# Where the first norm factor is applied, and how x is loaded and split, in a two-layer decoder step

## The reference, cut to what matters

```python
def rmsnorm(x, w):
    y = x * lax.rsqrt(jnp.mean(x * x, axis=-1, keepdims=True) + NORM_EPS)
    return y * w
...
h = rmsnorm(x, norm_w[0])                       # 320 tokens x 2048
proj = h @ w_in                                 # q, k, v, z and 2 x 32 gate columns
qkv, z, beta_raw, a_raw = jnp.split(proj, ...)
qkv = silu(causal_conv(qkv, cache, conv_w))     # width 4
o = gated_delta_rule(l2norm(q), l2norm(k), v, g(a_raw), sigmoid(beta_raw), state)
x = x + (rmsnorm(o) * silu(z)) @ w_out          # then the pooling layer and a last rmsnorm
```

## Time and profile before

| | |
|---|---|
| time, median of 3 runs | 2062.27 us |
| span of the profiled execution | 2061.9 us |
| TensorE (PE) busy | 2039.8 us, 99% |
| VectorE (DVE) busy | 1253.5 us, 61% |
| ScalarE (ACT) busy | 939.3 us, 46% |
| GpSimd (POOL) busy | 156.5 us, 8% |
| DMA, mean | 151 GB/s |

### The profile page before, as it was taken

One profiled execution on the slowest core, in us unless ns is written; L12 is line 12 of the kernel. 1 busy time (PEld: TensorE's weight loads), 2 busy tenths in 40 slices (PEclk: granted clock), 3 DMA queues, 4 the chain that ended last, 5 costly groups with the idle time before them and its releaser, 6 DMA issues.

```text
span 2061.9 us, 51677 instructions
## 1 busy us (share of the span) xinstructions
PE 2039.8 (99%) x19467; PEld 1959.5 (95%) x19467; DVE 1253.5 (61%) x2238; ACT 939.3 (46%) x2005; POOL 156.5 (8%) x354
## 2 busy tenths in 40 slices
PE   8999999999999999999999999999999999999998
PEld 7999999999999999999899999999999999999998
DVE  5766677776667776667754445555556556744433
ACT  5555555564555555455543334333333333433343
POOL 4101011010011101101100010000000000000010
PEclk9999999999999999999999999999999999999999
DMA  6544555554555554455555445454544445444443
GB/s 203 166 133 136 162 153 153 152 144 122 144 162 156 150 148 137 125 163 152 159 166 162 134 152 171 147 160 144 161 157 141 150 154 161 157 155 143 150 138 110
DMA packets 380491, 311.13 MB, mean 151 GB/s; under 512 B 19945, under 2 KB 377018, under 8 KB 379834
## 3 DMA queue, kind: packets, MB, share of 16 engines
q1 hardware_dynamic: 378554, 306.30, 49.0%
q10 hardware_dynamic: 1872, 3.96, 0.6%
HBM read 283.85 MB, written 27.25 MB: 151 GB/s over the span
## 4 chain that ended last, share of the span: by engine, by line
PE 93%; DVE 5%; issue 1%; ACT 0%; DVEq 0%; POOL 0%; ACTq 0%; POOLq 0%
PE ps L297 28%; PE ps L298 26%; PE ps L299 26%; PE ps L1227 10%; DVE s_s L1164 2%; PE ps L1382 2%; DVE wlo L288 1%; DVE silu L1019 1%; DVE silu L1017 1%; DVE amat L1174 1%; PE ps L1353 0%; DVE xlo L896 0%; PE ps L1356 0%; DVE sq L903 0%; PE ps L2030 0%
## 5 line engine op out<-in xcount | busy, mean ns | idle before, releaser
L297 PE MATMUL ps<-xhi,whi 128*128 128x320 f32 x3072 | 983.8, 320 | 5.8 <-DVE wlo L288 2.6
L299 PE MATMUL ps<-xhi,wlo 128*128 128x320 f32 x3072 | 949.6, 309 | 0.0
L298 PE MATMUL ps<-xlo,whi 128*128 128x320 f32 x3072 | 949.4, 309 | 0.0
L288 DVE TENSOR_TENSOR wlo<-wraw,whi 128x1024 fp32r<-128x1024 f32 (+1 forms) x484 | 579.1, 1217 | 240.2 <-ACT whi L283 237.7
L283 ACT ACTIVATE whi<-wraw 128x1024 fp32r<-128x1024 f32 (+1 forms) x484 | 498.0, 1050 | 307.8 <-PE ps L299 276.7
L297 PEld LDWEIGHTS ps<-xhi,whi 128*128 128x128 f32 x3072 | 577.4, 188 | 30.5 <-issue 15.9
L298 PEld LDWEIGHTS ps<-xlo,whi 128*128 128x128 f32 x3072 | 577.9, 188 | 0.9
L299 PEld LDWEIGHTS ps<-xhi,wlo 128*128 128x128 f32 x3072 | 577.3, 188 | 0.0
L297 PE MATMUL ps<-bhi,whi 128*128 128x320 f32 x512 | 157.7, 308 | 0.0
L298 PE MATMUL ps<-blo,whi 128*128 128x320 f32 x512 | 157.6, 308 | 0.0
L299 PE MATMUL ps<-bhi,wlo 128*128 128x320 f32 x512 | 157.6, 308 | 0.0
(11 more groups left out here) (352 smaller groups left out, 2048.1 us busy)
## 6 DMA issues: line engine op xcount, KB each, us to landing
wraw<-in_delta_w_in_dram SPq DMA_DIRECT2D x384, 256.0 KB, 3.0
wraw<-in_pool_w_in_dram SPq DMA_DIRECT2D x256, 256.0 KB, 3.0
wraw<-in_delta_w_out_dram SPq DMA_DIRECT2D x128, 256.0 KB, 3.3
wraw<-in_pool_w_out_dram SPq DMA_DIRECT2D x128, 256.0 KB, 3.3
s_s<-in_state_delta_dram SPq DMA_DIRECT2D x32, 512.0 KB, 6.2
out_dram<-s_s SPq DMA_DIRECT2D x32, 512.0 KB, 4.2
wraw<-in_pool_w_group_dram SPq DMA_DIRECT2D x64, 256.0 KB, 3.2
dec<-gc_rows SPq DMA_DIRECT2D x16, 320.0 KB, 4.0
```

The costliest lines, as they stand in the source:

```text
L288: nc.vector.tensor_tensor(wlo[:, slot, 0:width], wraw[:, slot, 0:width], whi[:, slot, 0:width].bitcast(F32), ALU.subtract).then_inc(E("w_l ...
L297: mm(o, whi[:, slot, w], hi[:, k_x, :], start=first, stop=False)
L298: mm(o, whi[:, slot, w], lo[:, k_x, :], start=False, stop=False)
L299: done = mm(o, wlo[:, slot, w], hi[:, k_x, :], start=False, stop=last)
```

## The change

It makes `xhi` on ScalarE straight from the turned tile in PSUM, scaled by the weight of the norm, and `xlo` on VectorE from `ht`, the weight and `xhi`; `sq` goes. `rb` is made behind the first eight k tiles of head 0 and multiplied where a projection leaves PSUM, for which `gfeat`, `qk_evac`, `v_evac` and `z_evac` become products on VectorE, at new places in its list. x is loaded in three pieces of columns, the small rows through ScalarE's DMA queue; the sums of squares stand between the tiles; GpSimd's constants for the level work wait for x; the gate chain stands four k tiles later, and VectorE's splits around it move. In the loop VectorE's last split of a turn (`split(11)`) moves behind the branch rows.

```diff
-    BY_DVE = (1, 3, 5, 7)
+    BY_ACT = (2, 4, 6, 8, 10, 12)
+    BY_DVE = (0, 1, 3, 5, 7, 9, 11, 13, 14, 15)
+    X_COLS = ((0, 4), (4, 10), (10, KT))
     def tile_bank(k):
...
-                "j (n c) -> (j n) c", c=P)).then_inc(E("rows_in"), 16)
-        sp.dma_start(gvec[:, 0, :], delta_a_log[0].partition_broadcast(P)).then_inc(E("rows_in"), 16)
-        sp.dma_start(gvec[:, 1, :], delta_dt_bias[0].partition_broadcast(P)).then_inc(E("rows_in"), 16)
+        for c, (c0, c1) in enumerate(X_COLS):
+            cols = slice(P * c0, P * c1)
+            sp.dma_start(xtok[:, 0, cols], x_prompt[0, 0:P, cols]).then_inc(E(f"x_in{c}"), 16)
+            sp.dma_start(xtok[:, 1, cols], x_prompt[0, P:2 * P, cols]).then_inc(E(f"x_in{c}"), 16)
...
         gp.tensor_copy(level[:], lv[:]).then_inc(E("c_all"), 1)
...
-            act.wait_ge(E("tiles_t"), k + 1)
-            sc.activation(ht[:, k, :], tile_bank(k)[:, 0:T], ACT.Copy).then_inc(E("act_tiles"), 1)
+        for s, r, n in ((norm_w.rearrange("n (k c) -> (n k) c", c=P), 0, 32),
...
+        act.wait_ge(E("vecs"), 1)
+        for k in range(KT):
+            act.wait_ge(E("tiles_t"), k + 1)
+            sc.activation(xhi[:, k, :], tile_bank(k)[:, 0:T], ACT.Copy, scale=vecs[:, k:k + 1]).then_inc(E("x_hi"), 1)
+            if k in BY_ACT:
+                sc.activation(ht[:, k, :], tile_bank(k)[:, 0:T], ACT.Copy).then_inc(E("act_tiles"), 1)
+            if k >= 12:
+                split_hi(act, k - 12, k - 12, 512)
+            if k in (6, 9, 12):
+                if k == 6:
+                    for c in range(len(X_COLS)):
+                        act.wait_ge(E(f"x_in{c}"), 48)
+                row_squares(k // 3 - 2)
+        split_hi(act, HEADS, 0)
+        act.wait_ge(E("act_tiles"), len(BY_ACT))
+        act.wait_ge(E("dve_tiles"), len(BY_DVE))
+        act.dma_start(ht_dram, ht[:].rearrange("p k t -> p (k t)")).then_inc(E("ht_saved"), 16)
...
-        for k in (2, 4, 6):
-            tile(k)
-        split_hi(act, 0, 0, 512)
-        for k in (8, 9, 10):
-            tile(k)
-        for k in range(KT):
-            if k + 11 < KT:
-                tile(k + 11)
-            if k in (2, 6, 10):
-                n = (k + 2) // 4
-                split_hi(act, n, n, 512)
-            if k == 8:
-                act.wait_ge(E("act_tiles"), 12)
-                act.wait_ge(E("dve_tiles"), 4)
-                act.dma_start(ht_dram, ht[:].rearrange("p k t -> p (k t)")).then_inc(E("ht_saved"), 16)
-            act.wait_ge(E("xnorm"), k + 1)
-            sc.activation(xhi[:, k, :], sq[:, k % 4, :], ACT.Copy).then_inc(E("x_hi"), 1)
-        split_hi(act, HEADS, 0)
-        for j in range(1, 4):
-            split_hi(act, HEADS + j, j)
...
+        for m in range(1, 4):
+            split_hi(act, HEADS + m, m)
...
-            act.wait_ge(E("w_used"), used)
-            if loop_of(i):
-                act.wait_ge(E("conv"), i * 16)
-            sc.activation(convin[:, 0:2, TAPS - 1:S_AT], ps[:, 0:2, 0:NPT], ACT.Copy)
-            sc.activation(conv_strips(convin, 0, 2, TAPS - 1, SLEN), toks(ps[:, 0:2, NPT:T]), ACT.Copy
-                          ).then_inc(E("qk_evac"), 1)
...
-        def z_evac(i, used):
-            act.wait_ge(E("z_half"), i + 1)
-            if loop_of(i):
-                act.wait_ge(E("gate"), i)
-            sc.activation(zraw[:, 0, :], ps[:, 0, 0:T], ACT.Copy)
-            act.wait_ge(E("w_used"), used)
-            sc.activation(zraw[:, 1, :], ps[:, 1, 0:T], ACT.Copy).then_inc(E("z_evac"), 1)
...
+        def low_x(k):
+            dve.wait_ge(E("x_hi"), k + 1)
+            tile_kept(dve, k)
+            v.scalar_tensor_tensor(xlo[:, k, :], ht[:, k, :], vecs[:, k:k + 1], xhi[:, k, :].bitcast(F32),
+                                   ALU.mult, ALU.subtract).then_inc(E("x_lo"), 1)
+        for k in range(KT):
+            if k in BY_DVE:
+                dve.wait_ge(E("x_hi"), k + 1)
+                v.tensor_copy(ht[:, k, :], tile_bank(k)[:, 0:T]).then_inc(E("dve_tiles"), 1)
+            if k >= 1:
+                low_x(k - 1)
+            if k >= 13:
+                split_lo(dve, k - 13, k - 13, 512)
+        low_x(KT - 1)
         dve.wait_ge(E("sumsq"), 3)
         v.tensor_scalar(small[:, 0:2], small[:, 3:5], 1.0 / DM, EPS, ALU.mult, ALU.add)
         v.tensor_scalar(small[0:64, 2:3], small[0:64, 5:6], 1.0 / DM, EPS, ALU.mult, ALU.add).then_inc(E("ms"), 1)
+        split_lo(dve, 3, 3, 512)
+        split_lo(dve, HEADS, 0)
         dve.wait_ge(E("rms"), 1)
         v.reciprocal(small[:, 9:11], small[:, 6:8])
         v.reciprocal(small[0:64, 11:12], small[0:64, 8:9]).then_inc(E("rinv"), 1)
...
+        last.then_inc(E("rms_row"), 1)
+        split_lo(dve, HEADS + 1, 1)
+        split_lo(dve, HEADS + 2, 2)
+        dve.wait_ge(E("row_ps"), 2)
+        v.tensor_copy(rb[:], D3[:, 0:T]).then_inc(E("rms_row"), 1)
+        dve.wait_ge(E("rms_row"), 2)
...
-        v.tensor_copy(gfeat[:], ps[:, 3, 0:T]).then_inc(E("g_in"), 1)
-        split_lo(dve, HEADS + 1, 1)
+        v.tensor_tensor(gfeat[:], ps[:, 3, 0:T], rb[:], ALU.mult).then_inc(E("g_in"), 1)
...
-        split_lo(dve, HEADS + 2, 2)
+        split_lo(dve, HEADS + 3, 3)
         dve.wait_ge(E("g_pe"), 1)
...
-        split_lo(dve, HEADS + 3, 3)
+        split_lo(dve, HEADS + 4, 0)
...
-        split_lo(dve, HEADS + 4, 0)
+        split_lo(dve, HEADS + 5, 1)
...
+        def evacuate(at, i, used, name):
+            dve.wait_ge(E("w_used"), used)
+            dve.wait_ge(E("conv_zero"), 1)
+            if not isinstance(i, int):
+                dve.wait_ge(E("tail"), i)
+            v.tensor_tensor(convin[:, at:at + 2, TAPS - 1:S_AT], ps[:, at:at + 2, 0:NPT],
+                            rb[:, 0:NPT].rearrange("p (o c) -> p o c", o=1).to_broadcast([P, 2, NPT]), ALU.mult)
+            for q in range(at, at + 2):
+                last = v.tensor_tensor(conv_strips(convin, q, q + 1, TAPS - 1, SLEN)[:, 0],
+                                       ps[:, q, NPT:T].rearrange("p (b s) -> p b s", s=SLEN),
+                                       rb[:, NPT:T].rearrange("p (b s) -> p b s", s=SLEN), ALU.mult)
+            last.then_inc(E(name), 1)
+        def qk_evac(i):
+            evacuate(0, i, i * 12 + (HEADS + 4), "qk_evac")
+        def v_evac(i):
+            evacuate(2, i, i * 12 + (HEADS + 8), "v_evac")
+        def z_evac(i):
+            dve.wait_ge(E("z_half"), i + 1)
+            if not isinstance(i, int):
+                dve.wait_ge(E("gate"), i)
+            v.tensor_tensor(zraw[:, 0, :], ps[:, 0, 0:T], rb[:], ALU.mult)
+            dve.wait_ge(E("w_used"), i * 12 + (HEADS + 12))
+            v.tensor_tensor(zraw[:, 1, :], ps[:, 1, 0:T], rb[:], ALU.mult).then_inc(E("z_evac"), 1)
...
-        split_lo(dve, HEADS + 5, 1)
+        split_lo(dve, HEADS + 6, 2)
...
         put(HBETA, ge)
+        qk_evac(0)
         dve.wait_ge(E("g_pe"), 3)
...
-        split_lo(dve, HEADS + 6, 2)
+        split_lo(dve, HEADS + 7, 3)
         dve.wait_ge(E("g_pe"), 4)
         v.tensor_copy(gcr[0:80, :], D1[0:80, 0:P]).then_inc(E("g_vec"), 1)
-        split_lo(dve, HEADS + 7, 3)
...
             v.scalar_tensor_tensor(gate[:], gate[:], 1.0, zraw[:], ALU.add, ALU.mult).then_inc(E("gate"), 1)
             split(3)
+            qk_next()
...
                     v.tensor_copy(xm[BL:64, :, 0:BL], blocks(D2[BL:64, 0:P], 4)).then_inc(E("x5"), 1)
                     split(8)
+            v_next()
...
             states(3)
             silus_next()
-            split(11)
+            z_next()
             dve.wait_ge(E("pe_round"), n + 1)
             b = branch[:, bass.ds(d * 2, 2), :]
             v.scalar_tensor_tensor(b[:, :, 0:NPT], blocks(D0, 2), vecs[:, V_O:V_O + 1], gate[:, :, 0:NPT], ALU.mult, ALU.mult)
             v.scalar_tensor_tensor(b[:, :, NPT:T], blocks(D1[:, 0:P], 2), vecs[:, V_O:V_O + 1], gate[:, :, NPT:T],
                                    ALU.mult, ALU.mult).then_inc(E("dve_round"), 1)
+            split(11)
...
         for half in range(2):
+            if half == 1:
+                split_lo(dve, HEADS + 10, 2)
+                split_lo(dve, HEADS + 11, 3)
             for j in range(TAPS):
                 conv(0, half, j)
-            for j in (10, 11) if half == 0 else range(12, 12 + LEAD):
-                split_lo(dve, HEADS + j, j % 4)
+            if half == 0:
+                v_evac(0)
+        for j in range(12, 12 + LEAD):
+            split_lo(dve, HEADS + j, j % 4)
         silus(0)
         decay_exponents(0)
+        z_evac(0)
...
+        pe.wait_ge(E("vrow_in"), 64)
+        tr(ps[:, 0, 320:321 + V_O], vrow[0:V_O + 1, :], ident[0:V_O + 1, 0:V_O + 1]).then_inc(E("row_ps"), 1)
         for k in range(KT):
...
                 tile_kept(pe, k - 5)
+                pe.wait_ge(E("x_hi"), k - 4)
...
-            if k == 4:
...
                 for h in range(2):
                     last = tr(ps[:, 2, P * h:P * h + P], crow[:, h, :], ident[:])
-            if k == 6:
```

(48 more changed lines are left out.)

96 lines of the change are left out of this document (25 added, 71 removed).

## The result

The changed kernel takes 2069.95 us (median of 6 runs, 2068.89 to 2070.89) against 2062.98 us (6 runs, 2061.71 to 2064.48): a ratio of 1.0032, 95% interval 1.0022 to 1.0041, so slower, by 7.0 us between the medians. The forecast was 2067.3 us, with a range of 2062 to 2071.5; the median lies 2.65 us above it. The profiled executions have spans of 2061.9 and 2067.2 us, 5.3 us apart; the kernel after is profiled in its fastest run (2068.89 us), so the rest of the 7.0 us is what executions of one kernel differ by. In later comparisons the kernel before has medians of 2063.63 to 2064.19 us, so a difference of medians that were not taken together is good to about 1 us. TensorE has as many matmuls as before (19467), behind longer waits.

The account below looks back on a forecast made before the run. TensorE bounds the loop, so only its waits at the start, head 0 and the last head can gain: +3.9 us up to head 1, +0.75 loop, +0.4 last head, +5.0 in all: 2067.3 us (8 in 10: 2062 to 2071.5).

Parts of the forecast that it names:

- T: Start of the first projection tile: from 40.11 to 38.5 us, 1.6 us earlier, with the clock low until 33.7 us.
- Rival 1: At the start the clock holds at 2.4 GHz through the gap, first projection tile at 36.3 us; 2065.1 us, chance 0.17.
- Piece 5: Head 0's projection: TensorE gets to piece 5 before VectorE's low part is done; a new wait of 1.5 us.
- gct: Head 0, turned cumulated gates: piece 7's low part no longer stands behind them, so TensorE's 1.51 us wait goes; -1.5.
- Tail: Head 0: v's evacuation on VectorE behind eight convolution steps makes the turned tail late; a new wait of 1.4 us.
- z at head 1: Head 1's first tile waits for z's evacuation, on VectorE behind silus and decay exponents; +3.1 us (2.4 to 3.5).
- Rival 2: VectorE catches up in head 0, so the wait at head 1 stays 0.5 us; 2064.2 us, chance 0.13.
- Loop: Head loop, 15 times: z's second half takes 0.49 instead of 0.43 us, 0.05 us each, 0.75 in all.
- Rival 5: In the loop VectorE is 0.8 us late for each next head's first tiles; +12, 2079 us, chance 0.07.
- Last head: The moved low part stands between the branch rows and the branch's first low part; +0.4 us (0 to 0.8).
- Rival 4: Lower clock lasts to 37 us, or the gates start 1.5 us later; 2068.8 to 2070 us, chance 0.14.
- Rival 3: All as the change would have it: full clock at the start, no new wait; 2059.1 us, chance 0.07.

Follow-up runs that it names:

- piece5_up: Changed kernel with ScalarE's high part of head 0's piece 5 ahead of its wait for the gate rows and the gate chain, instead of behind; 2067.26 us.
- v_up: Changed kernel with VectorE's products of head 0's v behind the first two of eight convolution instructions of the first half, instead of behind all eight; 2067.86 us.
- combo: Changed kernel with squares behind the tiles, piece 5's high part ahead of the gate chain, head 0's v behind two convolution steps, its z ahead of silus; 2056.42 us.
- combo_plus: combo plus, at head 0, z's evacuation between the low parts of pieces 12 and 13 and piece 10's high part ahead of the tail copies; 2056.27 us.

## Why the prediction was right, step by step

- **What bounds, and the result's sign**: right. TensorE is busy 199.55 of 200 us in the loop (199.76 before) and all of the loss but 1 us arises ahead of the transposes of head 1. In spans the size is right too (+5.3 for +5.0); the median is 2.65 us above the forecast and 0.95 above its own range of 2065.8 to 2069, inside the range of 2062 to 2071.5.
- **T**: right in direction, mis-sized. -2.98 us against -1.6, since the first gates matmul started at 27.98 and not 29.1 (ScalarE began at 12.07 us, not 12.9, and took 14.3 us for its list, not 14.6) and the clock was back at 32.5 us instead of 33.7. The gap was 4.5 us for "some 5". 0.5 us of the 2.98 is the start of the execution (first transposes at 11.38 instead of 11.89), which no edit made. Other executions had T at 36.69 to 39.00: my 38.5 lies in their spread, and so a part of this term is chance; in the earliest of them (piece5_up) the gates ended before 37 us, which I had called a sign of being wrong. Rival 1, the clock that holds, is out: at 24 to 25 us it is 0.50. But my reason, the gap, isn't what these rows show: the clock fell at 22.2 us, ahead of the gap of 4.51 us that began at 23.47, and in all seven executions with this start it fell (19.4 to 22.2 us) before that gap began, behind or within waits of 0.74 to 1.31 us among the transposes. The level was right, the cause that I named for it was not. Gaps send TensorE back to the lower clock, says the Trainium skill (TensorE: Matmul & The Clock Gate, "Why this matters for your kernels"); the trace agrees at head 1 (0.50 from 92 to 93 us, behind 3.92 us), while at the start the fall came behind waits shorter than those that the Trainium skill warns of there.
- **Row of roots behind T**: forecast +1.0; its six matmuls stand at 44.17 with 0.97 us, 8 tiles behind T.
- **Piece 5**: forecast +1.5, measured 1.36, and piece5_up shows its cause, ScalarE's place for the high part.
- **gct**: forecast -1.5, gone as said.
- **Tail**: forecast +1.4, measured 1.68; v_up shows the convolution steps ahead of v as the cause.
- **z at head 1**: forecast +3.1, measured 3.92 in place of 0.49, so +3.43, inside 2.4 to 3.5. Rival 2, VectorE that catches up, is out; its run had no gaps, as before. I had taken 0.2 us off for GpSimd's additions; those weren't saved.
- **The clock behind z**: missing in the forecast. The step that failed is the one that priced the wait of 3 to 4 us at its length alone. It cost 1.29 us more, and up to 2.46 in other executions.
- **Loop**: forecast +0.75 by 0.05 a turn; measured +0.75: 0.06 a turn in 13 turns, 0.05 less in the first. The step ahead of the next head's first tile has 0.05 of it, for the reason given. Rival 5 is out.
- **Last head**: forecast +0.4, measured +0.22.
- **Rival 4** (2068.8 to 2070) names the time that was measured, but not how: the gates started 1.1 us earlier than forecast, not 1.5 later, and the clock was back at 32.5 us, not 37.

In spans the sum was 0.3 us too low: the clock (1.3) and head 0 (0.6) cost more, T (1.4) and the last head (0.2) came out better than forecast. Two misses nearly cancelled, so the small error of the sum is partly luck. The rows from T to head 1 (0.97, 1.36, -1.51, 1.68, 3.43) make 5.93 of its 6.08 us; 0.15 us are not placed. Rival 3, that all goes as meant, took the change for free of new waits; combo shows what the change is worth when they are taken away (8 us less than before), with 5.9 us of it from the squares behind the tiles, which this rival didn't count.

## What to carry to other kernels

When an evacuation moves to another engine, its own length need not be the price (here 0.9 us, and 3.4 us of waiting); the price is what stands ahead of it in that engine's list, read from the producer's last matmul to the consumer's first. Put the instruction that the bottleneck waits for ahead of work that has slack, and check that what it displaces has some (combo_plus didn't). Before you call a removed wait lost to the next one, look whether the late engine itself waits for the bottleneck in between; if it does, the gain can be kept, as in piece5_up.
